# Banded attention in a two-block network: turned probabilities in two PSUM banks, and a new order of the work around them

## The reference, cut to what matters

```
s = einsum(q, k with the block before) ; s = where(in_window, s + bias, -inf)
m = max(max(s), sink) ; p = exp(s - m)
p = p / (sum(p) + exp(sink - m))
o_swa = einsum(p, v)
h = h + concatenate([o_gla, o_swa]) @ w_out
```

## Time and profile before

| | |
|---|---|
| median of 3 runs | 1549.02 us (1548.76 to 1549.63) |
| the profiled execution: its own time | 1549.25 us |
| its span, first to last instruction | 1547.4 us, mean granted TensorE clock 0.998 |
| PE busy | 1535.0 us (99%) |
| DVE, ACT, POOL busy | 980.9, 788.6, 905.6 us (63%, 51%, 59%) |

### The profile page before, as it was taken

How to read it: one execution, slowest core, us unless ns; L and a number is a source line. 1 busy time by engine, 2 the same in 40 slices (tenths; PEclk the granted TensorE clock), 3 DMA queues, 4 the chain that set the end, 5 groups by cost and what they waited for, 6 DMA issues and landing times.

```text
span 1547.4 us, 23342 instructions
## 1 busy us (share of the span) xinstructions
PE 1535.0 (99%) x8238; PEld 1273.0 (82%) x8238; DVE 980.9 (63%) x1795; ACT 788.6 (51%) x1399; POOL 905.6 (59%) x904
## 2 busy tenths in 40 slices
PE   9999999999999999999999999999999999999998
PEld 6777777777888888888887887788988899999986
DVE  5497986665235777667666445764333888888864
ACT  6435786554335544444444434653654656565643
POOL 6344664333554677777765542266544488888854
PEclk9999999999999999999999999999999999999999
DMA  5321221113222223322333321133322233333331
GB/s 202 100 96 68 82 95 69 64 59 109 95 98 100 92 93 109 109 96 95 110 113 105 123 85 52 55 123 108 110 96 96 82 99 107 99 107 100 106 109 69
DMA packets 46168, 150.37 MB, mean 97 GB/s; under 512 B 4648, under 2 KB 9904, under 8 KB 46064
## 3 DMA queue, kind: packets, MB, share of 16 engines
q1 hardware_dynamic: 39648, 140.00, 26.9%
q10 hardware_dynamic: 6416, 8.98, 1.7%
HBM read 146.73 MB, written 2.11 MB: 96 GB/s over the span
## 4 chain that ended last, share of the span: by engine, by line
PE 94%; DVE 3%; ACT 1%; DMA 1%; issue 1%; ACTq 0%; DVEq 0%
PE job L634 13%; PE job L636 13%; PE job L635 13%; PE score L980 6%; PE score L976 6%; PE job L959 5%; PE job L960 5%; PE job L961 5%; PE score L978 3%; PE score L979 3%; PE o L959 1%; PE o L960 1%; PE o L961 1%; PE o L912 1%; PE score L848 1%
## 5 line engine op out<-in xcount | busy, mean ns | idle before, releaser
L528 POOL TENSOR_TENSOR w_lo<-w_raw,w_hi 128x256 fp32r<-128x256 f32 x560 | 434.3, 808 | 446.1 <-ACT w_hi L1544 445.9
L534 POOL TENSOR_TENSOR w_lo<-w_raw,w_hi 128x512 fp32r<-128x512 f32 x218 | 294.3, 1366 | 170.8 <-ACT w_hi L1821 170.3
L634 PE MATMUL job<-a_hi,w_hi 128*128 128x512 f32 (+1 forms) x586 | 225.4, 385 | 0.1
L635 PE MATMUL job<-a_lo,w_hi 128*128 128x512 f32 (+1 forms) x586 | 221.4, 378 | 0.0
L636 PE MATMUL job<-a_hi,w_lo 128*128 128x512 f32 (+1 forms) x586 | 221.4, 378 | 0.0
L1544 ACT ACTIVATE w_hi<-w_raw 128x1024 fp32r<-128x1024 f32 x140 | 146.7, 1053 | 128.4 <-PE job L636 116.0
L1821 ACT ACTIVATE w_hi<-w_raw 128x512 fp32r<-128x512 f32 x218 | 133.6, 627 | 135.6 <-PE job L961 61.0
L2278 DVE TENSOR_TENSOR w_lo<-arena,w_hi 128x512 fp32r<-128x512 f32 x120 | 135.2, 1135 | 3.8 <-ACT w_hi L1821 3.2
L634 PEld LDWEIGHTS job<-a_hi,w_hi 128*128 128x128 f32 x586 | 110.2, 188 | 33.2 <-issue 9.6
L980 PE MATMUL score<-s_two,w_lo 128*128 128x256 f32 x480 | 135.3, 282 | 0.0
L634 PE MATMUL job<-b_two,w_hi 128*128 128x512 f32 x328 | 131.3, 400 | 0.0
(11 more groups left out here) (453 smaller groups left out, 3641.5 us busy)
## 6 DMA issues: line engine op xcount, KB each, us to landing
w_raw<-w_all SPq DMA_DIRECT2D x264, 512.0 KB, 3.2
arena<-x_t ACTq DMA_DIRECT2D x8, 512.0 KB, 6.2
out_t<-arena SPq DMA_DIRECT2D x6, 256.0 KB, 2.1
arena<-rg_w ACTq DMA_DIRECT2D x1, 1024.0 KB, 7.2
arena<-mem_t ACTq DMA_DIRECT2D x1, 1024.0 KB, 5.5
spare<-row_table ACTq DMA_DIRECT2D x3, 256.0 KB, 3.9
arena<-consts ACTq DMA_DIRECT2D x1, 512.0 KB, 3.5
out_t<-arena ACTq DMA_DIRECT2D x2, 256.0 KB, 2.5
```

Of the source, the lines that this page charges most:

```text
L528: nc.gpsimd.tensor_tensor(w_lo[:, sl, c], raw[:, sl, c], w_hi[:, sl, c].bitcast(F32), ALU.subtract).then_inc(s("lo_ready"), 1)
L534: nc.gpsimd.tensor_tensor(ff_tile(w_lo, tag), ff_source(tag), ff_tile(w_hi, tag).bitcast(F32), ALU.subtract).then_inc(s("ff_raw_low"), 1)
L634: mm(ps[:, 0:n], w_hi[:, sl, c], hi[:, kt, 0:n], start=kt == 0, stop=False)
L635: mm(ps[:, 0:n], w_hi[:, sl, c], lo[:, kt, 0:n], start=False, stop=False)
```

## The change

The turns with c = 0 go to bank `t_ps[0]` and those with c = 1 to bank `t_ps[1]`, the one that the values' product also uses. So a turn waits only for the copy of the turn two before it, and a turn with c = 1 also waits until DVE has made the rest of the values' result from that bank (`y2lo_ready`, `4 + t`). On PE each turn of a half now comes behind the half job's matmuls, and the two turns of a half stand together. On ACT `y2_high` comes ahead of `split`, and in round 0 the fourth turn is copied ahead of exp(1, 0). On DVE `y2_low(3 + t)` moves from behind `add_half(t - 1, 1)` to between inverse(t, 0) and inverse(t, 1), and in round 0 `add_half(0, 0)` comes ahead of max(1, 0).

```diff
             def swa_turn(t, half, c):
                 n = 4 * t + 2 * half + c
                 pe.wait_ge(s("swa_prob"), n + 1)
-                pe.wait_ge(s("swa_pt"), n)
+                if n >= 2:
+                    pe.wait_ge(s("swa_pt"), n - 1)
+                if c == 1 and t >= 1:
+                    pe.wait_ge(s("y2lo_ready"), 4 + t)
...
-                        ins = tp(t_ps[0][:, (b % 2 * 2 + e) * P:(b % 2 * 2 + e + 1) * P],
+                        ins = tp(t_ps[c][:, (b % 2 * 2 + e) * P:(b % 2 * 2 + e + 1) * P],
...
+                half_job(t, 0, (2, 3)).then_inc(s("half_done"), 1)
                 swa_turn(t, 0, 0)
-                half_job(t, 0, (2, 3)).then_inc(s("half_done"), 1)
                 swa_turn(t, 0, 1)
                 if t >= 1:
                     open_half(t, 1)
                     half_job(t, 1, (0, 1))
                 else:
                     half_job(t, 1, (2,))
+                half_job(t, 1, (2, 3) if t >= 1 else (3,)).then_inc(s("job_done"), 1)
                 swa_turn(t, 1, 0)
-                half_job(t, 1, (2, 3) if t >= 1 else (3,)).then_inc(s("job_done"), 1)
                 swa_turn(t, 1, 1)
...
-                       t_ps[0][:, first * P:T].rearrange("p (b c) -> p b c", c=P), ACT.Copy).then_inc(s("swa_pt"), 1)
+                       t_ps[c][:, first * P:T].rearrange("p (b c) -> p b c", c=P), ACT.Copy).then_inc(s("swa_pt"), 1)
...
             for t in range(4):
-                split(J_OUT2 + 3 + t)
-                if t >= 1:
+                if t == 0:
+                    split(J_OUT2 + 3)
+                else:
                     y2_high(3 + t)
+                    split(J_OUT2 + 3 + t)
                 take_turn(t, 0)
                 if t == 0:
-                    take_turn(t, 1, (0,))
+                    take_turn(t, 1)
                 if t < 3:
                     swa_exp(t + 1, 0)
-                take_turn(t, 1, (1,) if t == 0 else (0, 1))
+                if t > 0:
+                    take_turn(t, 1)
                 if t < 3:
                     swa_exp(t + 1, 1)
...
             for t in range(4):
                 if t >= 1:
                     swa_inverse(t, 0)
+                    y2_low(3 + t)
                 swa_inverse(t, 1)
                 if t >= 1:
                     add_half(t - 1, 1)
-                    y2_low(3 + t)
+                if t == 0:
+                    add_half(t, 0)
                 if t < 3:
                     swa_max(t + 1, 0)
-                add_half(t, 0)
+                if t > 0:
+                    add_half(t, 0)
                 if t < 3:
                     swa_max(t + 1, 1)
             add_half(3, 1)
```

## The result

| | before | changed |
|---|---|---|
| median (range, runs) | 1548.89 us (1548.65 to 1549.63, 6) | 1557.83 us (1554.5 to 1559.95, 6) |
| ratio of the runs | | 1.0056, 95% interval 1.0046 to 1.0066 |
| profiled execution: own time, span | 1549.25, 1547.4 us | 1554.5, 1552.7 us |

The kernel became slower, by 8.9 us between the medians (the ratio over matched runs says 8.7, within 7.1 to 10.2), where 2.8 was forecast. Two things stand out. The profiled execution, which is the fastest of the six, is 5.3 us slower in its span. And the six executions are spread over 5.5 us, where those of before lie within 1. Their mean granted TensorE clocks, in the order of their times, are 0.998 (1554.5 us), 0.997 (1556.56), 0.997 (1556.69), 0.996 (1558.96), 0.996 (1559.33) and 0.995 (1559.95): the slower, the lower.

A forecast was written before the change was run, and what follows sets the result against it. PE was taken to bound the kernel (94% of the chain). Removing 2.6 us but adding stalls of 2.2, 0.7 and 2.4 and an end of about 0.2 gave +2.8 to +2.9: 1551.8 us, range 1548.7 to 1554.0.

The forecast's parts named there:

- the three places and their releaser: PE idle before half_job(t, 1) near 978, 989 and 1000, released by DVE's addition; stalls of 2.2, 0.7 and 2.4 us.
- round 0's 1.54 us: PE goes on at 968.93 instead of 970.47 in round 0, 1.54 us ahead, all spent by round 1's stall.
- covered waits of the turns: Turns with c = 1 wait for y2_low, which is done 0.3 us or more before they come; costed at nothing.
- R1: Rival, chance 0.12: not slower, as DVE's additions come in time for PE; 1546.4 to 1548.2 us, say 1547.3.
- they take 2.0 to 2.2 to the next instruction: DVE's four multiplications of inverse(1, 1) in round 1, beside POOL's pieces, were claimed to take 2.0 to 2.2 us.
- the row of 966.00: Profile row before the change: DVE's four multiplications taking 2.28 us, read as POOL working through all of them.
- sum near +4.5: Total by the skill page's exclusive lock: four multiplications about 2.9 us, 0.8 more in rounds 1 and 3.
- The upper bound of 4.0: Largest slowdown: 2.9, plus 0.4 for multiplications at 2.2 in rounds 1 and 3, plus 0.7 for one more POOL piece.
- R3: Rival, chance 0.04: PE's clock falls at the 2.2 and 2.4 us stalls, 2 x 2.7 us more, about 1557.
- (a): In round 0, DVE's addition put ahead of max(1, 0) removes a PE stall of 1.35 us.
- (b): Two banks for the turns remove PE's waits for the copy of the turn ahead, 0.91 us.
- (c): Turns side by side on PE save about one switch of 0.08 us in each of four rounds, 0.3 us.

The follow-up runs named there:

- the version in which all stalls of rounds 1 to 3 are gone: Changed kernel with add_half(t - 1, 1) ahead of y2_low and inverse(t, 1), and ACT's split behind the copies of half 0, in rounds 1 to 3: 1546.99 us.

## Why the prediction was wrong

**The steps that held.** The direction; the three places and their releaser; round 0's 1.54 us won and spent; y2_low waiting for ACT, and the wait for the values in rounds 2 and 3; POOL starting with the multiplications; covered waits of the turns; nothing given back behind the stretch (the starts of the last values differ by 5.3, as the spans do). R1 did not come about; its upper time of 1548.2 doesn't follow from its own words either, as half of 2.6 gives 1547.7.

**The step that failed** is the size of one term: "they take 2.0 to 2.2 to the next instruction". They take 3.0 in each of the three rounds. The number came from the row of 966.00, called "the same four instructions under the same four pieces". It was not: POOL had started at 964.83, so 1.17 us and with it the first piece and nearly half of the second were over, and the last multiplication ran alone behind 967.87. The rows of before, taken apart as above:

```profile
966.44 0.84 DVE L2282 TENSOR_SCALAR arena<-arena,small 128x256 f32<-128x256 f32 x1
966.44 1.58 DVE L2282 TENSOR_SCALAR arena<-arena,small 128x256 f32<-128x256 f32 x2
967.94 0.34 DVE L2282 TENSOR_SCALAR arena<-arena,small 128x256 f32<-128x256 f32 x1
...
964.83 1.60 POOL L528 TENSOR_TENSOR w_lo<-w_raw,w_hi 128x256 fp32r<-128x256 f32 x2 [10.52 <-ACT w_hi L1544]
966.39 1.47 POOL L528 TENSOR_TENSOR w_lo<-w_raw,w_hi 128x256 fp32r<-128x256 f32 x2
```

The right reading is one piece of POOL (0.72 to 0.75 us) for each multiplication that starts while a piece runs: 4 x 0.75 = 3.0; for the row of 966.00, three pieces that end at about 966.4, 967.1 and 967.9, and one multiplication alone, 2.2 to 2.3; for the one of 973.75 (POOL from 974.33), the fourth waits for the first piece, 1.5. All three come out. That is what the Trainium skill says in "SBUF — State Buffer" (section on the two separate sides of SBUF), an exclusive lock for a whole instruction; the prediction set it beside the rows (2.9 us, sum near +4.5) and took the row. The traces agree with the rule in all three rounds, and so does the row once it is read rightly. The sum of +4.5 was itself too low: it added 0.8 us in rounds 1 and 3 only, and with round 2 it would have been +5.3.

With 3.0 in place of 2.1 the stalls are 0.9 longer in each round: 2.2, 0.7 and 2.4 become 3.1, 1.6 and 3.3 (measured 3.0, 1.5, 3.2), and the sum 2.85 + 3 x 0.9 = 5.5 (measured 5.7 by the stretch, 5.3 by the spans). This error alone takes the time out of the stated range: the execution that kept its clock took 1554.5 us, and the range ended at 1554.0. The upper bound of 4.0 was wrong for the same reason: it let the error be passed on once, not in every round, though each round's addition is behind its own multiplications.

**The second failure** is R3, the clock, held at a chance of 0.04. It is what moved the median from 1554.5 to 1557.8, as the version with PE kept at work shows: there the spread is gone and the time is 1554.7. That R3's own price, about 1557, lies near the measured median is chance: it was a sum of 2.8 and two losses of 2.7, and the measured one is 5.3 and some 3.3. In the prediction the stalls were up to 2.4 us; the earlier trace rows bracket the fall between 1.16 us idle of 4.5 and a far emptier end, and a gap near 3 was not excluded. Its price was put at 2.7 us a stall, as if all four tiles ran at the lower level; in the traced execution only a part of them did (granted clock 0.58 and then 0.85 behind the first stall), and the falls cost 1.5 and 1.6. The slowest of the six lost 5.5 in all, and what it is made of is open. The prediction read the Trainium skill's "TensorE: Matmul & The Clock Gate" (section on oscillation) as allowing stalls of 2.2 and 2.4 us. In no run did this stage have stalls of that length; the clock fell around idle times of 2.76 and 2.96 us, so the runs neither bear out that reading nor refute it. What decides whether it falls in a given execution is open: two executions of one program, with stalls of the same length, differ.

**Parts.** (a) was priced at 1.35 for itself; alone it is worth nothing (1549.13 against 1549.29). (a), (b) and (c) together, 2.6 us, were about the right size: the version in which all stalls of rounds 1 to 3 are gone gains 2.3. (b) and (c) were not measured by themselves.

## What to carry to other kernels

When an instruction is set beside another engine's work with which it shares a lock, count the pieces it will meet from the start times of both, one piece for each instruction; a duration from a row where the overlap was partial is no bound, and an error in it comes back in every round that has such a place. Ask of every instruction that frees a buffer for the bottleneck engine what is queued ahead of it: the same slow multiplications cost 5.3 us with both additions behind them (1554.5 against 1549.2) and about 1 us with the first one ahead (1547.9 against 1547.0). And when a change makes the bottleneck's stalls grow to some 3 us, look at the spread of the runs and at the granted clock of each, not only at the profiled execution, which may be the one that kept its clock.

## What the runs showed of the hardware that was not expected

- A VectorE multiplication by a per-partition scalar (alone 0.29 us for 128x128, 0.35 for 128x256) did not end until just after the GpSimd piece that ran when it started: four took 3.00 to 3.07 us beside pieces of 0.73 to 0.77, and 1.07 alone. GpSimd itself was hardly slowed (2.87 to 2.93 us for four pieces, 2.81 to 2.84 clear of the multiplications).
- In one traced execution TensorE's granted clock fell to its lower level (1.2 GHz) around idle times of 2.76 and 2.96 us and stayed at the upper one around 1.29 us; in another, with the same idle times, it never fell there. Two times 2.8 us of repeated matmuls in the long gaps, useless in themselves, made the whole kernel 2.0 us faster.
